# Set-up's segments placed anew, and one sum of the last inner pair rounded by itself, in a two-block transformer kernel

## Chip, cores and metric

One Trainium2 chip; the kernel runs on 1 of its cores. The metric is the device time of one execution in microseconds (us). Each core has TensorE (PE; PEld is its weight load), VectorE (DVE), ScalarE (ACT), GpSimd (POOL) and the DMA queues (SP's above all).

## What is computed

Two model blocks in a row over 512 tokens (plus 16 meta tokens in the first), width 1024. All of it is fp32; the parts that matter here are the square-ReLU MLPs, the gated feed-forward, and the set-up of a state-space filter:

```python
def _sq_relu_mlp(h, w_up, w_down):        # first block, two layers, 4096 inner
    u = jax.nn.relu(h @ w_up)
    return (u * u) @ w_down
# first block: h = h + mixer(rmsnorm(h)); h = h + _sq_relu_mlp(rmsnorm(h), w_up[i], w_down[i])
# second block: attention in three groups, a state-space filter (state 64, 32 groups of 16),
#   a gated feed-forward with 2816 inner, gated embeddings, rmsnorm
```

The state-space filter's tables (powers of a complex decay times B and times C, in chunks of 8 tokens) depend on parameters only. They are computed once, inside the first layer's MLP, where VectorE has room; that is the "set-up".

## The kernel before, in words

**Precision by two halves.** Each fp32 operand is split in a rounded part (`_hi`, fp32r) and the rest (`_lo`); a product is three matmuls, hi by hi, hi by lo, lo by hi (L1303 to L1305). For each unit of weights (128x1024) ACT writes `w_hi` (L2041) and POOL subtracts to get `w_lo` (L1072). For each inner tile of an MLP DVE takes the ReLU out of PSUM (L3670, L3642), ACT squares and rounds it, and DVE subtracts to get the low part (`inner_low`, L3676; `low_inner`).

**The first layer's MLP.** `up00` makes 16 inner tiles (m = 0 to 15), `down00` uses them for 8 output tiles, two units of weights each. PE works tile after tile, with two PSUM banks in turn: tile m + 2 can't start before DVE has taken tile m out of its bank. In `down00`'s first tile PE waits, k by k, for `hidden_lo`, the low part of inner tile k.

**Set-up.** `ssm_setup` (from L3259) is a Python generator of DVE instructions, cut by `yield` into segments. `hidden` (in DVE's `mlp`) emits, for each tile m of `up00`, the ReLU, then one or two segments, then `inner_low`; `plain`, for each tile of `down00`, adds the tile to the residual (L3687) and then emits some segments. DVE carries them out in that written order. Numbered from 0, the segments are: 0 to 10 parameters and angles; 11 to 13 the powers `a_n`; 14 and 15 the table `bb`; 16 to 19 twelve full-width operations (128x1024, three in a segment) that make `pw_re` and `pw_im`, with `ssm_tab` told at the end of 19; 20 the kernel table `kern`; then three with nothing in them (21 to 23); 24 to 35 twelve more full-width operations, one each, that write `pw_re` and `pw_im` again, for C, with `ssm_tab` told after 35; 36 to 38 the powers `a_pow` of the eighth power (small operations). PE waits for segment 19 ahead of `kernel_products`, which it does after `down00`'s tile 1, and DVE in segment 24 waits for PE's transposes of `pw` (`turn_powers`), the last of which follow tile 5. After `down00` comes `first_part`, ten inner tiles whose ReLUs are L3642.

In `up00` tiles 11, 12 and 13 have two segments (11+12, 13+14, 15+16), all other tiles one, so that 17 stands in tile 14 and 18 in tile 15. In `down00`, tiles 0 to 4 have one, tile 5 four (24 to 27), tile 6 five, tile 7 six (33 to 38).

**Down projections by seven products.** Five stretches (parts 0 to 4; the sizes are 10, 12, 12, 10 and 12 inner tiles) do their down projection by a seven-product scheme (Strassen-Winograd) on 2x2 blocks: the inner tiles come in pairs, and a quad is two output tiles, so each part has four quads. The products are called P1, P2, P5, P6, P3, P4, P7, in the order in which PE does them. Inputs on the activation side are seven forms: three are halves of the inner tiles (forms 0 to 2, low parts told by `hidden_lo`), and four are sums s1 to s4 of a pair (forms 3 to 6). DVE makes s1 to s4 (L3564, L3565, L3567, L3568, 128x256 each, or 128x264 in part 0), ACT rounds all four in one instruction (L2434, `sums_high`), and DVE subtracts all four in one (L3556, `sums_low`), which tells `sums_lo`. P5 reads form 3 (s1), P6 reads form 4 (s2), P4 form 2, P7 form 5 and P3 form 6.

In a part's first quad the last pair has only just been made. PE does P1 whole, then P2 and P5 but for the last pair, then P2's last pair, then P5's last pair, then P6 and the others whole. `ready` is the wait for one pair of a product; it is called for P1, P2 and P5 only. DVE's order there is: s1 to s4, the low part of the last inner tile (L3575 or L3579), `keep(P1)` (adds PSUM to the residual, L3550), `sums_low`, `product_low(P6)` (L3531, the low part of the weights of P6), `keep(P2)` and so on. In parts 3 and 4 `product_low(P5)` stands between s4 and the low part. The low weights of P3 and P4 are subtracted on POOL (L1133) after ACT's rounding (L2429).

```python
project(by_name["up00"], hidden)
project(by_name["down00"], plain)
assert not list(setup)
# hidden: for _ in range(2 if m in (11, 12, 13) else 1): next(setup)
# plain:  for _ in range({5: 4, 6: 5, 7: 6}.get(m, 1)): next(setup)
```

Of the kernel before, what the change touches and what calls it, by code (L numbers as in the profile page):

```python
# [48 lines left out]
P1, P2, P5, P6, P3, P4, P7 = range(7)  # L49
# [209 lines left out]
def transposed_blocks_program(nc, a, out):  # L259
# [96 lines left out]
    with ctx:  # L356
# [178 lines left out]
        with ExitStack() as s:  # L535
# [31 lines left out]
            "hidden_full", "hidden_hi", "hidden_lo",  # L567
            "block0", "block1", "block2", "block3", "block4", "block5",
            "weight_sum", "product_hi", "product_lo", "product_lo_pool", "product", "product_kept",
            "pair_sums", "sums_hi", "sums_lo",  # L570
            "gate", "gated", "mixed_hi", "mixed_lo",
            "a_hi", "a_lo", "negmax", "exp", "inverse", "factor", "recip", "last_recip", "eps_rows", "scaled", "probs", "p_full", "p_stored", "metas",
            "dve", "act",
# [49 lines left out]
        def forms_of(part):  # L623
            return (form_hi, form_lo) if part else (first_hi, first_lo)

        def sums_of(part):
            return pair_sums if part else sums_first
# [194 lines left out]
        def bc(t, n):  # L822

            return bass.AP(t.tensor, t.offset, [list(x) for x in t.ap] + [[0, n]])
# [327 lines left out]
        def _(pe):  # L1152
# [500 lines left out]
            def down_by_products(part):  # L1653
# [4 lines left out]

                def ready(i, k):
                    form = PRODUCTS[i][1]  # L1660
                    if form > 2:
                        pe.wait_ge(sems["sums_lo"], FIRST_PAIR[part] + k + 1)
                    else:
                        pe.wait_ge(sems["hidden_lo"], T.at("hidden_lo", 2 * pairs - 1 - 2 * k - (form > 0)))
# [27 lines left out]
                def high(q, i, ks):  # L1692
                    hi, form = weights_of(q, i)[0], PRODUCTS[i][1]
                    opens = i in (P1, P2, P5, P4)
                    for k in ks:
                        if q.first and i in (P1, P2, P5):
                            ready(i, k)
                        mm(region(q, i), hi[:, k, :], forms_hi[:, form, k, :], start=opens and k == 0, stop=False,  # L1698
                           skip_group_check=not opens)
                        mm(region(q, i), hi[:, k, :], forms_lo[:, form, k, :], start=False, stop=False,  # L1700
                           skip_group_check=not opens)
# [323 lines left out]
        def _(act):  # L2025
# [405 lines left out]
            def sums_high(part, j):  # L2431

                act.wait_ge(sems["pair_sums"], FIRST_PAIR[part] + j + 1)
                fn(forms_of(part)[0][:, 3:7, j, :], sums_of(part)[:], ACT.Copy).then_inc(sems["sums_hi"], 1)  # L2434

            def round_inner(part, pair, m):

# [21 lines left out]
            def by_products(part, pj, duty, first=None):  # L2459

                own = [q for q in QUADS if q.part == part]
                instead[BEHIND[part]] = lambda: product_high(own[0], P2)
                project(pj, duty, first=first, carry=True)
                product_high(own[0], P5)
                left_over.pop(0)()
                sums_high(part, PART_SIZES[part] // 2 - 1)
                for q in own:
                    for i in range(7):
                        if not q.first or i > P5:
                            product_high(q, i)  # L2470
                        if part == LAST_PART and i == P5 and not q.first:
                            round_residual(q.before)
                        if q is QUADS[-1] and i == P4:
                            round_p()
                act.wait_ge(sems["product"], own[-1].done(P7) - 2)
                round_unit(BEHIND[part])
                held[BEHIND[part] + 1] = own[-1].done(P7) - 1
                if part == LAST_PART:
                    round_residual(own[-1])
# [406 lines left out]
        def _(dve):  # L2886
# [3 lines left out]
            def step(ins):  # L2890

                ins.then_inc(sems["dve"], T.up("dve"))
                dve.wait_ge(sems["dve"], T.at("dve"))
# [365 lines left out]
            def ssm_setup():  # L3259
# [82 lines left out]
                for part in range(2):  # L3342
# [15 lines left out]
                dve.wait_ge(sems[f"o_full{o}"], T.at(f"o_full{o}"))  # L3358
                v.tensor_tensor(kern[:], ops_[o][:], skip, ALU.add).then_inc(
                    sems[f"o_stored{o}"], T.up(f"o_stored{o}"))  # L3360
                for _ in range(4):
                    yield
                for _ in range(8):
                    others(T, "t_")
# [9 lines left out]
                                yield  # L3374
                v.memset(p(23), 0.0).then_inc(sems["ssm_tab"], T.up("ssm_tab"))
                yield

                pr, pi = a_pow[:, 0], a_pow[:, 1]
                step(v.tensor_copy(pr[:, :, 0:1], re[:, :, 8:9]))
                step(v.tensor_copy(pi[:, :, 0:1], im[:, :, 8:9]))  # L3380
                for n in (1, 2, 4):
                    for _ in product_ops(pr[:, :, n:2 * n], pi[:, :, n:2 * n], pr[:, :, 0:n], pi[:, :, 0:n],
                                         bc(pr[:, :, n - 1], n), bc(pi[:, :, n - 1], n),
                                         *(x[:, :, 0:n] for x in small_t)):
                        pass
                    yield

            setup = ssm_setup()

# [162 lines left out]
            def sums_low(part, j):  # L3552

                dve.wait_ge(sems["sums_hi"], FIRST_PAIR[part] + j + 1)
                hi, lo = forms_of(part)
                v.tensor_tensor(lo[:, 3:7, j, :], sums_of(part)[:], hi[:, 3:7, j, :].bitcast(F32),  # L3556
                                ALU.subtract).then_inc(sems["sums_lo"], 1)

            def sums_of_pair(part, pair):

                t1, t2 = halves_of(part)
                a11, a21, a12, a22 = pair[:, 0, t1], pair[:, 0, t2], pair[:, 1, t1], pair[:, 1, t2]
                s1, s2, s3, s4 = (sums_of(part)[:, n, :] for n in range(4))
                v.tensor_tensor(s1, a21, a22, ALU.add).then_inc(sems["dve"], T.up("dve"))  # L3564
                v.tensor_tensor(s3, a11, a21, ALU.subtract).then_inc(sems["dve"], T.up("dve"))  # L3565
                dve.wait_ge(sems["dve"], T.at("dve", 1))
                step(v.tensor_tensor(s2, s1, a11, ALU.subtract))  # L3567
                v.tensor_tensor(s4, a12, s2, ALU.subtract).then_inc(sems["pair_sums"], 1)  # L3568

# [29 lines left out]
            def by_products(part):  # L3599

                for q in QUADS:
                    if q.part != part:
                        continue
                    if q.first:
                        keep(q, P1)
                        sums_low(part, PART_SIZES[part] // 2 - 1)
                    else:
                        product_low(q, P2)
                        product_low(q, P5)
                        keep(q, P1)  # L3610
                        weight_sum(q, "T4")
                        if part == LAST_PART:
                            low_residual(q.before)
                    product_low(q, P6)
                    keep(q, P2)
                    keep(q, P5)
                    then = None if q.last else QUADS[q.g + 1]
                    keep(q, P6)
                    if then:
                        weight_sum(then, "T3")  # L3620
                    product_low(q, P7)
                    keep(q, P3)
                    if q is QUADS[-1]:
                        low_p()
                    if then:
                        weight_sum(then, "T1")
                        product_low(then, P1)
                    keep(q, P4)
                    if then:
                        weight_sum(then, "T2")  # L3630
                    keep(q, P7)
                    if q is QUADS[-1]:
                        low_residual(q)

            def inner_part(part, pj, pair, banks, factor):
# [3 lines left out]
                def hidden(m, s, t, b):  # L3639
# [6 lines left out]
                    T.saw("hidden_hi")  # L3646
                    if m % 2:
                        dve.wait_ge(sems["hidden_full"], T.at("hidden_full"))
                        sums_of_pair(part, pair)
                    elif m:  # L3650
                        sums_low(part, m // 2 - 1)
                    low_inner(part, pair, m)
# [13 lines left out]
            def mlp():  # L3666
# [11 lines left out]

                def hidden(m, s, t, b):
                    inner(m, s, b)  # L3680
                    for _ in range(2 if m in (11, 12, 13) else 1):
                        next(setup)
                    inner_low(m, s)

                def plain(m, s, t, b):
                    dve.wait_ge(sems[f"full{b}"], T.at(f"full{b}"))
                    store(v.tensor_tensor(h[:, m, :], h[:, m, :], acc1[b], ALU.add), b)  # L3687
                    for _ in range({5: 4, 6: 5, 7: 6}.get(m, 1)):
                        next(setup)

                def hidden_left(m, s, t, b):
# [1 line left out]
                    inner_low(m, s)  # L3693

                project(by_name["up00"], hidden)
                project(by_name["down00"], plain)
                assert not list(setup)
                for name in ("ends_out0", "ends_out1"):
# [457 lines left out]
            for part, pj in ((FFN_PART, ffn_in), (LAST_PART, ffn_rest)):  # L4156
                ahead, tiles = QUADS[part * DT // 2], PART_SIZES[part]

                def ffn(m, s, t, b):
# [10 lines left out]
                        return  # L4170
                    if m % 2:
                        dve.wait_ge(sems["hidden_full"], T.at("hidden_full"))
                        sums_of_pair(part, pair_ffn)
                    if m == tiles - 1:
                        product_low(ahead, P5)
                    low_inner(part, pair_ffn, m)
# [86 lines left out]
```

## Time and profile before

| | |
|---|---|
| median of 3 runs | 2099.0 us (2098.72 to 2099.3) |
| the profiled execution's own time | 2097.7 us |
| its span, first to last instruction | 2095.9 us |
| mean granted TensorE clock | 0.998 |
| PE / PEld / DVE / ACT / POOL busy | 2074.5 / 1819.8 / 1404.1 / 895.7 / 815.2 us |
| HBM traffic over the span | 101 GB/s |

A time in a row is counted from the span's start. A matmul row has its start, its modelled duration, the source line and the operands; matmuls are pipelined, so the distance between two starts, not the duration, says how fast PE issues. A bracket at the end gives the engine's idle time ahead of the instruction and what ended it.

### The profile page before, as it was taken

Reading aid. Unit: us, or ns where it says so; the run is one execution under the profiler, and the core shown is the slowest. Engines: PE = TensorE matmul, PEld = TensorE weight load, DVE = VectorE, ACT = ScalarE, POOL = GpSimd, SP = SyncE. Lnnn points to the kernel's source line nnn. Section 1 sums busy time; section 2 is a strip of 40 time slices with the busy share of each in tenths; the row PEclk is TensorE's granted clock in tenths of the full one; section 3 lists DMA queues with packets and bytes.
Section 4 is the critical chain, followed back from the end, with each engine's and each line's share of the span. In section 5 each row is a group of like instructions: output and inputs, shape, how many; then the busy total and the mean of one; then the engine's idle time right before and its main releaser. Section 6 shows DMA issues by size and latency. Waiting matters only on the chain.

```text
span 2095.9 us, 34962 instructions
## 1 busy us (share of the span) xinstructions
PE 2074.5 (99%) x14218; PEld 1819.8 (87%) x14218; DVE 1404.1 (67%) x2172; ACT 895.7 (43%) x1479; POOL 815.2 (39%) x388
## 2 busy tenths in 40 slices
PE   9999999999999999999999999999999999999998
PEld 9998899999999777798898788888888788988897
DVE  6678766628746395685855769566674577666865
ACT  5368644223435393443434433344433433433344
POOL 3343434344234454423334443333444443344332
PEclk9999999999999999999999999999999999999999
DMA  6620245244233602334343465233333332433341
GB/s 178 169 59 2 57 136 148 84 133 136 73 100 106 188 2 80 102 84 109 81 121 92 131 137 161 67 88 86 91 89 92 91 94 79 120 92 101 89 120 64
DMA packets 375827, 211.23 MB, mean 101 GB/s; under 512 B 27043, under 2 KB 368260, under 8 KB 374776
## 3 DMA queue, kind: packets, MB, share of 16 engines
q1 hardware_dynamic: 365358, 192.62, 32.9%
q10 hardware_dynamic: 10314, 16.41, 2.9%
q8 instruction: 113, 1.85, 0.4%
q14 instruction: 42, 0.34, 0.1%
HBM read 196.97 MB, written 15.40 MB: 101 GB/s over the span
## 4 chain that ended last, share of the span: by engine, by line
PE 62%; issue 22%; POOL 10%; DVE 5%; ACT 1%; DMA 0%; POOLq 0%; SPq 0%; DVEq 0%; ACTq 0%
PE acc L1303 13%; PE acc L1304 13%; PE acc L1305 13%; POOL w_lo L1072 9%; PE acc L1393 2%; PE acc L1708 2%; PE acc L1698 2%; PE acc L1700 2%; PE ops L1462 2%; PE tps L1708 1%; PE tps L1700 1%; PE tps L1698 1%; PE ops L1698 1%; DVE tmp_s L3203 1%; PE ops L1700 1%
## 5 line engine op out<-in xcount | busy, mean ns | idle before, releaser
L1072 POOL TENSOR_TENSOR w_lo<-raw,w_hi 128x1024 fp32r<-128x1024 f32 x270 | 662.0, 2452 | 938.7 <-ACT w_hi L2041 928.2
L2041 ACT ACTIVATE w_hi<-raw 128x1024 fp32r<-128x1024 f32 x269 | 284.8, 1059 | 779.1 <-PE acc L1305 748.5
L1303 PE MATMUL acc<-hr_hi,w_hi 128*128 128x512 f32 x1056 | 421.6, 399 | 0.5 <-DVE qkv L3853 0.3
L1305 PE MATMUL acc<-hr_hi,w_lo 128*128 128x512 f32 x1056 | 417.7, 396 | 0.0
L1304 PE MATMUL acc<-hr_lo,w_hi 128*128 128x512 f32 x1056 | 417.6, 395 | 0.0
L1303 PE MATMUL acc<-hn_hi,w_hi 128*128 128x264 f32 (+1 forms) x840 | 246.8, 294 | 3.3 <-DVE pair_first L3642 2.9
L1305 PE MATMUL acc<-hn_hi,w_lo 128*128 128x264 f32 (+1 forms) x840 | 244.2, 291 | 0.0
L1304 PE MATMUL acc<-hn_lo,w_hi 128*128 128x264 f32 (+1 forms) x840 | 244.2, 291 | 0.0
L1303 PEld LDWEIGHTS acc<-hr_hi,w_hi 128*128 128x128 f32 x1056 | 198.5, 188 | 49.2 <-issue 1.4
L1305 PEld LDWEIGHTS acc<-hr_hi,w_lo 128*128 128x128 f32 x1056 | 198.4, 188 | 47.7
L1304 PEld LDWEIGHTS acc<-hr_lo,w_hi 128*128 128x128 f32 x1056 | 198.5, 188 | 47.3 <-issue 0.7
L1303 PEld LDWEIGHTS acc<-hn_hi,w_hi 128*128 128x128 f32 x840 | 158.2, 188 | 6.6 <-DVE pair_first L3642 3.1
L1304 PEld LDWEIGHTS acc<-hn_lo,w_hi 128*128 128x128 f32 x840 | 158.3, 188 | 2.7
L1305 PEld LDWEIGHTS acc<-hn_hi,w_lo 128*128 128x128 f32 x840 | 157.5, 188 | 2.5
L1303 PE MATMUL acc<-mid_hi,w_hi 128*128 128x264 f32 x352 | 100.6, 286 | 3.9 <-DVE mid_lo L3676 3.2
L1304 PE MATMUL acc<-mid_lo,w_hi 128*128 128x264 f32 x352 | 99.7, 283 | 0.0
L1305 PE MATMUL acc<-mid_hi,w_lo 128*128 128x264 f32 x352 | 99.7, 283 | 0.0
L1133 POOL TENSOR_TENSOR w_lo<-blocks,w_hi 128x768 fp32r<-128x768 f32 (+1 forms) x24 | 44.2, 1848 | 139.0 <-ACT w_hi L2429 139.0
L2429 ACT ACTIVATE w_hi<-blocks 128x768 fp32r<-128x768 f32 (+1 forms) x72 | 58.9, 823 | 86.7 <-PE acc L1708 26.4
L2193 ACT ACTIVATE probs<-probs,stat 128x528 f32<-128x528 f32 (+2 forms) x132 | 85.2, 646 | 13.7 <-DVE stat L3019 13.0
L1095 POOL TENSOR_SCALAR probs<-probs,stat 128x528 f32<-128x528 f32 (+2 forms) x49 | 65.4, 1335 | 61.6 <-DVE stat L3008 61.6
L1303 PEld LDWEIGHTS acc<-mid_hi,w_hi 128*128 128x128 f32 x352 | 66.3, 188 | 4.7 <-DVE mid_lo L3676 3.7
(606 smaller groups left out, 4628.0 us busy)
## 6 DMA issues: line engine op xcount, KB each, us to landing
raw<-in_w_up SPq DMA_DIRECT2D x64, 512.0 KB, 4.9
raw<-in_w_in SPq DMA_DIRECT2D x56, 512.0 KB, 3.8
raw<-in_w_down SPq DMA_DIRECT2D x24, 512.0 KB, 3.7
blocks<-in_w_down SPq DMA_DIRECT2D x32, 384.0 KB, 3.7
raw<-in_w_ffn_gate SPq DMA_DIRECT2D x22, 512.0 KB, 3.8
raw<-in_w_ffn_up SPq DMA_DIRECT2D x22, 512.0 KB, 3.8
raw<-in_w_in_even SPq DMA_DIRECT2D x18, 512.0 KB, 6.9
blocks<-in_w_ffn_down SPq DMA_DIRECT2D x16, 384.0 KB, 3.6
```

What stands on the lines that cost most here:

```text
L1072: nc.gpsimd.tensor_tensor(w_lo[:, part], raw[:, slot], w_hi[:, part].bitcast(F32), ALU.subtract).then_inc(sems["lo"], T.up("lo"))
L1095: nc.gpsimd.tensor_scalar(S, S, st[:, 4:5], None, ALU.mult).then_inc(sems["scaled"], T.up("scaled"))
L1133: nc.gpsimd.tensor_tensor(lo, block_of(q, PRODUCTS[i][0]), hi.bitcast(F32), ALU.subtract).then_inc(sems["product_lo_pool"], 1)
L1303: mm(out, w_hi[:, part, w0 + k, :], xh, start=s0, stop=False)
L1304: mm(out, w_hi[:, part, w0 + k, :], xl, start=False, stop=False)
L1305: ins = mm(out, w_lo[:, part, w0 + k, :], xh, start=False, stop=s1)
L1698: mm(region(q, i), hi[:, k, :], forms_hi[:, form, k, :], start=opens and k == 0, stop=False, skip_group_check=not opens)
L1700: mm(region(q, i), hi[:, k, :], forms_lo[:, form, k, :], start=False, stop=False, skip_group_check=not opens)
L1708: ins = mm(region(q, i), lo[:, k, :], forms_hi[:, form, k, :], start=False, stop=k == pairs - 1, skip_group_check=not opens)
L2041: fn(w_hi[:, n % 2], raw[:, n % 4], ACT.Copy).then_inc(sems["hi"], T.up("hi"))
L2193: fn(S, S, ACT.Exp, bias=st[:, o:o + 1], scale=-1.0, accum_out=p.den(st, o)).then_inc(sems["exp"], T.up("exp"))
L2429: fn(weights_of(q, i)[0], block_of(q, role), ACT.Copy).then_inc(sems["product_hi"], 1)
```

## The change

It has two parts that have nothing to do with each other.

**Set-up.** The segments of `a_pow` (36 to 38) move ahead of the second twelve full-width operations, into the places of segments 21 to 23, which had nothing in them, and the last three places go away. In `up00` tile 13 has one segment instead of two; one segment is emitted between `up00` and `down00`; in `down00` tiles 5, 6 and 7 have 5, 4 and 3 segments. So `up00`'s tile 13 has 15 alone, tile 14 has 16, tile 15 has 17, segment 18 stands after tile 15's `inner_low`, tile 0 has 19 and tile 1 has 20 as before, tiles 2 to 4 have `a_pow`, tiles 5 to 7 the twelve operations, by 5, 4 and 3.

**The last pair's first sum.** For the last pair of each part s1 tells a semaphore of its own (`late_sum`); ACT rounds it by itself (`late_high`) ahead of the other three, and DVE subtracts it by itself (`late_low`), in `by_products` ahead of `keep(P1)`. `sums_high` and `sums_low` of that pair take the other three only. P5's last pair waits for `late_lo`, and P6, in a first quad, now waits pair by pair for `sums_lo`.

```diff
                 def ready(i, k):
                     form = PRODUCTS[i][1]
-                    if form > 2:
+                    if form == 3 and k == pairs - 1:
+                        pe.wait_ge(sems["late_lo"], part + 1)
+                    elif form > 2:
                         pe.wait_ge(sems["sums_lo"], FIRST_PAIR[part] + k + 1)
...
-                        if q.first and i in (P1, P2, P5):
+                        if q.first and i in (P1, P2, P5, P6):
                             ready(i, k)
...
             def sums_high(part, j):
 
                 act.wait_ge(sems["pair_sums"], FIRST_PAIR[part] + j + 1)
-                fn(forms_of(part)[0][:, 3:7, j, :], sums_of(part)[:], ACT.Copy).then_inc(sems["sums_hi"], 1)
+                n = 1 if j == PART_SIZES[part] // 2 - 1 else 0
+                fn(forms_of(part)[0][:, 3 + n:7, j, :], sums_of(part)[:, n:4], ACT.Copy).then_inc(sems["sums_hi"], 1)
+
+            def late_high(part):
+
+                act.wait_ge(sems["late_sum"], part + 1)
+                fn(forms_of(part)[0][:, 3, PART_SIZES[part] // 2 - 1, :], sums_of(part)[:, 0], ACT.Copy).then_inc(
+                    sems["late_hi"], 1)
...
                 left_over.pop(0)()
+                late_high(part)
                 sums_high(part, PART_SIZES[part] // 2 - 1)
...
             def sums_low(part, j):
 
                 dve.wait_ge(sems["sums_hi"], FIRST_PAIR[part] + j + 1)
-                hi, lo = forms_of(part)
-                v.tensor_tensor(lo[:, 3:7, j, :], sums_of(part)[:], hi[:, 3:7, j, :].bitcast(F32),
+                (hi, lo), n = forms_of(part), 1 if j == PART_SIZES[part] // 2 - 1 else 0
+                v.tensor_tensor(lo[:, 3 + n:7, j, :], sums_of(part)[:, n:4], hi[:, 3 + n:7, j, :].bitcast(F32),
                                 ALU.subtract).then_inc(sems["sums_lo"], 1)
 
-            def sums_of_pair(part, pair):
+            def late_low(part):
+
+                (hi, lo), j = forms_of(part), PART_SIZES[part] // 2 - 1
+                dve.wait_ge(sems["late_hi"], part + 1)
+                v.tensor_tensor(lo[:, 3, j, :], sums_of(part)[:, 0], hi[:, 3, j, :].bitcast(F32),
+                                ALU.subtract).then_inc(sems["late_lo"], 1)
+
+            def sums_of_pair(part, pair, late=False):
...
+                if late:
+                    v.tensor_tensor(s1, a21, a22, ALU.add).then_inc(sems["late_sum"], 1)
+                    v.tensor_tensor(s3, a11, a21, ALU.subtract).then_inc(sems["dve"], T.up("dve"))
+                    dve.wait_ge(sems["late_sum"], part + 1)
...
                     if q.first:
+                        late_low(part)
                         keep(q, P1)
                         sums_low(part, PART_SIZES[part] // 2 - 1)
...
-                for _ in range(4):
+                yield
+
+                pr, pi = a_pow[:, 0], a_pow[:, 1]
+                step(v.tensor_copy(pr[:, :, 0:1], re[:, :, 8:9]))
+                step(v.tensor_copy(pi[:, :, 0:1], im[:, :, 8:9]))
+                for n in (1, 2, 4):
...
                     yield
                 for _ in range(8):
                     others(T, "t_")
...
-                    for _ in range(2 if m in (11, 12, 13) else 1):
+                    for _ in range(2 if m in (11, 12) else 1):
                         next(setup)
...
-                    for _ in range({5: 4, 6: 5, 7: 6}.get(m, 1)):
+                    for _ in range({5: 5, 6: 4, 7: 3}.get(m, 1)):
                         next(setup)
...
                 project(by_name["up00"], hidden)
+                next(setup)
                 project(by_name["down00"], plain)
```

The old `a_pow` code at the generator's end is taken out, and the two callers of `sums_of_pair` pass `m == tiles - 1` as `late`.

## Rows read from the trace of the kernel before

**Rows 1.** The page, part 1: busy time, share of the span, instructions

```profile
PE 2074.5 (99%) x14218; PEld 1819.8 (87%) x14218; DVE 1404.1 (67%) x2172; ACT 895.7 (43%) x1479; POOL 815.2 (39%) x388
```

**Rows 2.** Waits of PE over the span: total us, times, longest us

```profile
PE acc L1303 <- DVE mid_lo L3676: 3.2, 2, 2.7
PE acc L1303 <- DVE pair_first L3642: 2.9, 1, 2.9
...
PE acc L1303 <- DVE hid L3670: 0.6, 1, 0.6
```

**Rows 3.** Timeline of PE from up00's end to first_part: start us, duration us

```profile
377.61 0.28 PE L1305 MATMUL acc<-hn_hi,w_lo 128*128 128x264 f32 x1
378.51 0.39 PE L1303 MATMUL acc<-mid_hi,w_hi 128*128 128x264 f32 x1 [0.63 <-DVE hid L3670]
...
389.36 0.28 PE L1305 MATMUL acc<-mid_hi,w_lo 128*128 128x264 f32 x1
392.32 0.39 PE L1303 MATMUL acc<-mid_hi,w_hi 128*128 128x264 f32 x1 [2.68 <-DVE mid_lo L3676]
...
404.85 0.43 PE L1582 MATMUL ops<-pw_re,ct_re 128*32 128x128 f32 x8
...
495.02 0.39 PE L1303 MATMUL acc<-hn_hi,w_hi 128*128 128x264 f32 x1 [2.89 <-DVE pair_first L3642]
```

**Rows 4.** Timeline of DVE, 371 to 400 us: set-up's full-width operations

```profile
371.28 2.48 DVE L3203 TENSOR_TENSOR tmp_s<-bb,a_n 128x1024 f32<-128x1024 f32 x2
373.80 3.30 DVE L3203 TENSOR_TENSOR pw_re<-tmp_s 128x1024 f32<-128x1024 f32 x1
...
391.56 0.71 DVE L3676 TENSOR_TENSOR mid_lo<-hid,mid_hi 128x528 fp32r<-128x528 f32 x1
...
398.56 1.22 DVE L3203 TENSOR_TENSOR pw_im<-tmp_s 128x1024 f32<-128x1024 f32 x1
```

**Rows 5.** Timeline of POOL, at the second of those rows

```profile
373.27 2.75 POOL L1072 TENSOR_TENSOR w_lo<-raw,w_hi 128x1024 fp32r<-128x1024 f32 x1 [3.22 <-ACT w_hi L2041]
```

**Rows 6.** Timeline of DVE at down00's end and first_part's start

```profile
487.14 0.16 DVE L3379 COPY a_pow<-a_n 128x16 f32<-128x16 f32 x1
...
494.26 0.71 DVE L3642 SCALAR_TENSOR_TENSOR pair_first<-acc,rstd 128x528 f32<-128x528 f32 x1 [0.23 <-DVE a_pow L3203]
```

**Rows 7.** Timeline of PE in the first quads of parts 0, 3 and 4

```profile
546.53 0.29 PE L1708 MATMUL tps<-first_hi,w_lo 128*128 128x264 f32 x1
547.36 0.39 PE L1698 MATMUL ops<-first_hi,w_hi 128*128 128x264 f32 x1 [0.54 <-DVE first_lo L3556]
...
1784.29 0.28 PE L1708 MATMUL tps<-form_hi,w_lo 128*128 128x256 f32 x1
1785.41 0.39 PE L1698 MATMUL ops<-form_hi,w_hi 128*128 128x256 f32 x1 [0.85 <-DVE form_lo L3556]
...
1970.92 0.28 PE L1708 MATMUL tps<-form_hi,w_lo 128*128 128x256 f32 x1
1971.21 0.39 PE L1698 MATMUL ops<-form_hi,w_hi 128*128 128x256 f32 x1
```

**Rows 8.** Timeline of DVE in the first quad of part 3

```profile
1783.21 0.69 DVE L3575 TENSOR_TENSOR form_lo<-hid,form_hi 128x512 fp32r<-128x512 f32 x1
1783.81 0.41 DVE L3550 TENSOR_TENSOR h<-h,acc 128x256 f32<-128x256 f32 x1
1784.14 1.22 DVE L3556 TENSOR_TENSOR form_lo<-pair_sums,form_hi 128x1024 fp32r<-128x1024 f32 x1
1785.28 0.82 DVE L3531 TENSOR_TENSOR third_lo<-blocks,third_hi 128x640 fp32r<-128x640 f32 x1
```

**Rows 9.** Timelines of ACT and POOL in the same quad

```profile
1782.59 1.06 ACT L2434 ACTIVATE form_hi<-pair_sums 128x1024 fp32r<-128x1024 f32 x1 [0.96 <-DVE pair_sums L3568]
...
1785.48 3.58 POOL L1133 TENSOR_TENSOR w_lo<-blocks,w_hi 128x640 fp32r<-128x640 f32 x2 [13.59 <-ACT w_hi L2429]
```

**Rows 10.** Waits of all engines: ACT on a DMA of raw weights

```profile
ACT w_hi L2041 <- DMA raw<-in_w_up: 9.4, 3, 4.1
```

More of the change, by code:

```diff
@@ L569, in transposed_blocks_program @@
             "weight_sum", "product_hi", "product_lo", "product_lo_pool", "product", "product_kept",
-            "pair_sums", "sums_hi", "sums_lo",
+            "pair_sums", "sums_hi", "sums_lo", "late_sum", "late_hi", "late_lo",
             "gate", "gated", "mixed_hi", "mixed_lo",
@@ L3360, in ssm_setup @@
                     sems[f"o_stored{o}"], T.up(f"o_stored{o}"))
-                for _ in range(4):
+                yield
[3 more added lines that the diff above has]
+                for n in (1, 2, 4):
+                    for _ in product_ops(pr[:, :, n:2 * n], pi[:, :, n:2 * n], pr[:, :, 0:n], pi[:, :, 0:n],
+                                         bc(pr[:, :, n - 1], n), bc(pi[:, :, n - 1], n),
+                                         *(x[:, :, 0:n] for x in small_t)):
+                        pass
                     yield
@@ L3376, in ssm_setup @@
                 yield
[L3378 to L3386, printed above, removed]
             setup = ssm_setup()
@@ L3563, in sums_of_pair @@
                 s1, s2, s3, s4 = (sums_of(part)[:, n, :] for n in range(4))
-                v.tensor_tensor(s1, a21, a22, ALU.add).then_inc(sems["dve"], T.up("dve"))
-                v.tensor_tensor(s3, a11, a21, ALU.subtract).then_inc(sems["dve"], T.up("dve"))
-                dve.wait_ge(sems["dve"], T.at("dve", 1))
+                if late:
+                    v.tensor_tensor(s1, a21, a22, ALU.add).then_inc(sems["late_sum"], 1)
+                    v.tensor_tensor(s3, a11, a21, ALU.subtract).then_inc(sems["dve"], T.up("dve"))
+                    dve.wait_ge(sems["late_sum"], part + 1)
+                else:
+                    v.tensor_tensor(s1, a21, a22, ALU.add).then_inc(sems["dve"], T.up("dve"))
+                    v.tensor_tensor(s3, a11, a21, ALU.subtract).then_inc(sems["dve"], T.up("dve"))
+                    dve.wait_ge(sems["dve"], T.at("dve", 1))
                 step(v.tensor_tensor(s2, s1, a11, ALU.subtract))
@@ L3648, in hidden @@
                         dve.wait_ge(sems["hidden_full"], T.at("hidden_full"))
-                        sums_of_pair(part, pair)
+                        sums_of_pair(part, pair, m == tiles - 1)
                     elif m:
@@ L4172, in ffn @@
                         dve.wait_ge(sems["hidden_full"], T.at("hidden_full"))
-                        sums_of_pair(part, pair_ffn)
+                        sums_of_pair(part, pair_ffn, m == tiles - 1)
                     if m == tiles - 1:
```

## The prediction

> **What bounds the kernel now.** The page's busy times come first: PE is busy for 2074.5 of 2095.9 us [rows 1], everything else far less. So a change pays only where it takes away a wait of PE, and the next view is the list of PE's waits. Three of its entries belong to set-up: PE waited for `mid_lo` (2.7 us of the 3.2 in one wait), for `pair_first` (2.9) and for `hid` (0.6) [rows 2]. Each is DVE being late, and the timeline shows where [rows 3]. At 378.51 us `down00`'s first matmul waits for the ReLU of `up00`'s tile 14 to leave its bank. At 392.32 the low part of inner tile 15, the last, is awaited. At 495.02 `first_part`'s third tile waits for the ReLU of its first. The true cost of a wait is the distance between starts less the usual one of 0.12 us: 378.51 - 377.61 - 0.12 = 0.78; 392.32 - 389.36 - 0.12 = 2.84; for the third I take the bracket, 2.89, plus the 0.16 by which the other two exceed theirs, 3.05. Together 6.67 us.
>
> The timeline of the first quads gives the other part [rows 7]: P5's last pair starts 0.71 us late in part 0 (547.36 - 546.53 - 0.12), 1.00 in part 3, 0.17 in part 4. In parts 1 and 2 I found no such gap. Together 1.88 us, so 8.55 us of PE's waiting are in reach.
>
> **Why DVE is late in set-up.** From 371 us on, DVE has no idle time. A full-width operation takes 1.22 to 1.24 us alone (2.48 for two; 1.22), but 3.30 when it meets POOL [rows 4]: it began at 373.80 inside POOL's subtraction of 373.27 and ended at 377.10, 1.08 after POOL had ended at 376.02 [rows 5]. So a segment of three costs 3.70 us, and 2.1 more for each meeting. There is one POOL subtraction per unit of weights, every 5.8 us or so while PE isn't held up. The Trainium skill ("SBUF — State Buffer", section on the two separate sides) says that the pair of ports shared by the two engines is held for a whole instruction by whichever began first, and the other fully blocks; by that rule the operation would end at 376.02 + 1.22 = 377.24, and the trace agrees within 0.14 us.
>
> **The queue after the change, step by step.** Tile 14 of `up00` is full at about 371.95 (tile 15 ends at 377.61 + 0.12, less a tile of 5.8). DVE by then has only done segment 15. From 371.95 its order is ReLU 14, segment 16, low 14, ReLU 15, segment 17, low 15, segment 18, addition of tile 0, segment 19. A ReLU, a low part or an addition takes 0.65 to 0.71 [rows 4, 6]; I count 0.65, since instructions overlap a little.
> - ReLU 15: 371.95 + 0.65 + 3.70 + 2.1 + 0.65 + 0.65 = 379.7. The ReLU of tile 14, for which `down00` waited, is done at 372.6: 0.78 us are gone. `down00`'s first tile starts at 377.73.
> - Low 15: 379.7 + 3.70 + 0.65 and two meetings (POOL's subtractions near 379 and 385) = 388.2. PE wants it at 392.32 - 2.84 - 0.78 = 388.7. It comes 0.5 us early, so the 2.84 are gone, narrowly.
> - Segments 18 and 19: 388.2 + 7.40 + 0.65 and two meetings = 400.5. `kernel_products` started at 404.85 [rows 3] and would now want `ssm_tab` at 404.85 - 3.62 = 401.2. It fits by 0.7 us.
>
> That last margin is a wait that the change moves: segment 19 stays in tile 0, but 18 is now queued ahead of it there. Behind both, DVE's additions of tiles 1 and 2 have a whole tile of some 12 us each.
>
> **The tail of set-up.** DVE now ends the last tile's segments with the `a_pow` ones, from 487.14 to the ReLU at 494.26 [rows 6]: 7.1 us, which go to tiles 2 to 4, where segments had nothing in them and DVE does only a 0.7 us addition per tile. Tiles 5, 6, 7 hold the same twelve operations, one more in tile 5, one fewer in 6 and the same three in 7. The ReLU comes at about 487.3 (less all shifts), and PE, which would reach that tile at 495.02 - 3.05 = 492.0, needs its bank 4 us after the ReLU is done. The 3.05 us are gone in full. What is late next: nothing by these rows; ACT squares this tile right behind.
>
> The extra instructions of the placement are none: it only moves them. Set-up's sum: -6.67.
>
> **The first sum by itself.** Added per part are one ACT instruction, one DVE instruction, their waits, and PE's waits ahead of P6's pairs. ACT sat idle for 0.96 us ahead of the rounding of the four sums [rows 9]. A rounding a quarter as wide as its 1.06 us fits there, so I cost it at nothing. If that cover went, it would cost at most 1.06. On DVE a 256-wide operation advances the queue by 0.33 (1783.81 to 1784.14), a 1024-wide one by 1.14 (1784.14 to 1785.28) [rows 8]; each further 256 of width by (1.14 - 0.33) / 3 = 0.27, so three quarters of the width by 0.33 + 2 x 0.27 = 0.87. In part 3:
> - `late_low` 1783.81 to 1784.22; P5's last pair is wanted at 1784.29 + 0.12 = 1784.41. The 1.00 is gone.
> - `keep(P1)` 1784.14 to 1784.56, wanted by P6's opening at 1784.76 + 0.12 = 1784.88.
> - `sums_low` of three 1784.47 to about 1785.4; P6 wants its last pair at 1784.88 + 8 x 0.12 = 1785.8.
> - `product_low(P6)` from 1785.34, ending 0.82 later at 1786.16. P6's low weights are now wanted at 1784.88 + 10 x 0.12 = 1786.1: a new wait of some 0.1 us, and what was 1.00 yields 0.9.
>
> In parts 0 and 4 the same steps leave 0.4 us or more at each place (there PE was late by less), so 0.71 and 0.17. In parts 1 and 2 I count nothing. PE's new waits for pairs made long ago: P5 has them already and issues at 0.12 all the same, so nothing. Sum: -1.78.
>
> **Forecast.** -6.67 - 1.78 = -8.45 against the profiled execution's 2097.7, that is 2089.3. The median shown is 1.3 above that execution, so 2099.0 - 8.4 = **2090.6 us**. A measurement of this kernel can tell about 0.2% (4.2 us) from no change.
>
> **Rivals.**
> 1. *DVE's queue takes one meeting more.* The margins of 0.5 and 0.7 us are smaller than one meeting, 2.1. Then `mid_lo` is awaited for 1.6 us, or `kernel_products` for 1.4, or both in part: 2092.2. For it: DVE had no idle time there. Against: meetings are bound to POOL's subtractions, one each 5.8 us, and I counted five of them. Chance 0.13.
> 2. *The first sum gives nothing*, since the wait moves from P5 to P6's opening, or `late_high` isn't ahead of the rest on ACT after all: 2099.0 - 6.7 = 2092.3. Against it: the steps above. Chance 0.07.
> 3. *The time comes back later*, at something not paced by PE. ACT waited 9.4 us in three waits for a DMA of raw weights [rows 10]; if arrivals in a later stage were set by the memory and not by freed buffers, PE would run into them 8 us earlier. With 5 to 8 us given back: 2095.6 to 2099. Against it: the DMAs move 101 GB/s over the span and are issued as buffers come free. Chance 0.07.
> 4. *The port goes to POOL first, and the kernel is slower.* In part 3 DVE began `product_low(P6)` at 1785.28 and POOL its subtractions at 1785.48 [rows 8, 9]. By my steps DVE now begins at 1785.34. The point that decides is a further 0.14 us: if POOL begins first, DVE ends 0.82 after POOL's 1.8 (one subtraction) or 3.58 (both), so PE waits 2.0 or 3.8 us. In part 3 alone that gives 2090.6 + 2 to 4 = 2092.6 to 2094.5. In all five parts with both subtractions it gives 5 x 3.8 = 19 against the 6.7 of set-up: 2111, slower. Chance 0.06 for one part, 0.02 for enough of them to be slower than before. The same section of the skill makes this rival possible: by its rule whoever begins first decides, and the sum above is the case in which DVE does.
>
> **How the numbers follow.** The forecast has what is left, 0.65, with its own range of 2089.6 to 2092.0 (all waits gone with nothing new: 2099.0 - 8.55 = 2090.4, and 0.8 below that for wake-ups after a wait that I left out and for the spread of runs; upwards the two narrow margins). Rivals 1 and 2 and the one-part case of 4 lie up to 2094.5, so the range 2089.6 to 2094.6 holds all but rival 3 and the slower case. Faster by over 0.2% means below 2094.8: 0.65 + 0.13 + 0.07 + 0.06 = 0.91. Within 0.2%: 0.07. Slower: 0.02.
>
> **What would show it.** In the changed kernel's list of PE's waits `hid`, `mid_lo` (but for the 0.5 us of the second wait) and `pair_first` should be gone, and those for `form_lo` and `first_lo` too. `kernel_products` should start at about 401.2 and `down00`'s first matmul at 377.7. The small `a_pow` operations should lie in `down00`'s tiles 2 to 4. In part 3 PE should show a gap of at most 0.2 us ahead of P6's low products, with DVE's subtraction begun before POOL's. I am wrong if PE's wait for `ssm_tab` or for the low weights of P6 exceeds 1 us, or if a wait that isn't in the list of before takes more than 1 us anywhere.

## The result and the profile after

The changed kernel takes 2087.6 us (median of 5; 2086.9 to 2087.8), the one before 2099.0 (2098.7 to 2099.3): 11.4 us or 0.54% less between the medians; the ratio over all runs is 0.9944 with a 95% interval of 0.9931 to 0.9958, which doesn't take in 1. The forecast was 2090.6 with a range of 2089.6 to 2094.6: the sign was right, the time lies 2 us below the range. The profiled execution took 2087.2, its span is 2085.4.

The changed kernel's list of PE's waits, whole (total us, times, longest us), against [rows 2]:

```profile
PE ops L1990 <- DVE sq L4247: 1.9, 1, 1.9
PE acc L1491 <- DVE sq_tok L3113: 1.1, 1, 1.1
PE acc L1393 <- issue: 0.9, 1, 0.9
PE acc L1303 <- DVE mid_lo L3698: 0.6, 1, 0.6
PE ops L1434 <- DVE mix_e_lo L3071: 0.5, 2, 0.3
PE tps L1402 <- ACT probsT L2208: 0.5, 1, 0.5
PE acc L1303 <- POOL w_lo L1072: 0.5, 2, 0.3
PE acc L1235 <- DVE hn_lo L3130: 0.3, 1, 0.3
PE tps L1402 <- issue: 0.2, 1, 0.2
```

`pair_first`, `hid` and the long `mid_lo` are gone, and so are `form_lo` and `first_lo`. PE at the places of [rows 3]: `down00`'s first matmul, its last k, that is the product with inner tile 15 (389.36 and 392.32 before), and `kernel_products`.

```profile
376.84 0.29 PE L1303 MATMUL acc<-mid_hi,w_hi 128*128 128x264 f32 x1
...
387.59 0.28 PE L1305 MATMUL acc<-mid_hi,w_lo 128*128 128x264 f32 x1
387.71 0.28 PE L1303 MATMUL acc<-mid_hi,w_hi 128*128 128x264 f32 x1
...
400.13 0.43 PE L1582 MATMUL ops<-pw_re,ct_re 128*32 128x128 f32 x8
```

PE now passes the last k at its usual 0.12 us. `down00` starts 0.89 us ahead of the 377.73 that the forecast had, and `kernel_products` 1.1 ahead of its 401.2; 0.9 of it was gained before `down00` begins, at two places that no change touched (below). DVE in the same stretch, against [rows 4] (start us, duration us):

```profile
371.86 4.56 DVE L3213 TENSOR_TENSOR tmp_s<-bb,a_n 128x1024 f32<-128x1024 f32 x2
376.46 1.22 DVE L3213 TENSOR_TENSOR pw_re<-tmp_s 128x1024 f32<-128x1024 f32 x1
...
378.96 4.06 DVE L3213 TENSOR_TENSOR tmp_s<-bb,a_n 128x1024 f32<-128x1024 f32 x2
...
384.32 2.79 DVE L3698 TENSOR_TENSOR mid_lo<-hid,mid_hi 128x528 fp32r<-128x528 f32 x1
387.03 2.47 DVE L3213 TENSOR_TENSOR tmp_s<-bb,a_n 128x1024 f32<-128x1024 f32 x2
...
391.42 3.94 DVE L3213 TENSOR_TENSOR tmp_s<-bb,a_n 128x1024 f32<-128x1024 f32 x2
395.40 1.23 DVE L3213 TENSOR_TENSOR pw_im<-tmp_s 128x1024 f32<-128x1024 f32 x1
396.70 0.07 DVE L3359 MEMSET par<- 128x16 f32 x1
```

The low part of tile 15 is done at 387.11 and wanted at 387.71: 0.6 us to spare, where the forecast had 0.5. Segment 19 ends at 396.77 and is wanted at 400.13: 3.4 to spare instead of 0.7. Most of the difference is in the meetings with POOL, which cost 2.1, 1.6, 2.1, 0 and 1.5 us (4.56 - 2.48, 4.06 - 2.48, 2.79 - 0.71, 0, 3.94 - 2.48) and not five times 2.1. The 0 is POOL's subtraction of 389.78, which began inside a DVE operation: there POOL waited, taking 3.25 us instead of about 2.4.

The first quad of part 3, against [rows 7, 8, 9]: DVE, POOL and PE.

```profile
1774.39 0.42 DVE L3572 TENSOR_TENSOR form_lo<-pair_sums,form_hi 128x256 fp32r<-128x256 f32 x1
1774.73 0.41 DVE L3559 TENSOR_TENSOR h<-h,acc 128x256 f32<-128x256 f32 x1
1775.06 0.95 DVE L3565 TENSOR_TENSOR form_lo<-pair_sums,form_hi 128x768 fp32r<-128x768 f32 x1
1775.92 0.82 DVE L3540 TENSOR_TENSOR third_lo<-blocks,third_hi 128x640 fp32r<-128x640 f32 x1
...
1776.07 3.63 POOL L1133 TENSOR_TENSOR w_lo<-blocks,w_hi 128x640 fp32r<-128x640 f32 x2 [13.62 <-ACT w_hi L2431]
...
1774.87 0.28 PE L1710 MATMUL tps<-form_hi,w_lo 128*128 128x256 f32 x1
1774.98 0.28 PE L1700 MATMUL ops<-form_hi,w_hi 128*128 128x256 f32 x1
...
1776.40 0.28 PE L1702 MATMUL acc<-form_lo,third_hi 128*128 128x256 f32 x1
1776.80 0.85 PE L1710 MATMUL acc<-form_hi,third_lo 128*128 128x256 f32 x5
```

P5's last pair follows at 0.11 us where it was 1.00 late. DVE began P6's low weights 0.15 us ahead of POOL. They ended at 1776.74, so PE started on them 0.28 us late (1776.80 - 1776.40 - 0.12), and lost 0.24 more in the matmuls behind.

**Where the traces differ.** I paired every matmul of the one trace with the same matmul of the other and read the difference of their starts. It grows by 0.88 at `down00`'s start, 2.95 at its last k, 3.15 in `first_part` (7.0 for set-up); by 0.8 in part 0, 0.1 in parts 1 and 2, 0.6 net in part 3 (1.12 less 0.52), 0.3 in part 4 (1.8 for the sums). That is 8.8 us at the forecast's places, for 8.45 forecast. Another 1.7 lies where no instruction was changed or moved: 0.4 in the first 13 us, 0.5 at 343 us (a wait for POOL), 0.6 at 1282 us, 0.2 between 1800 and 1831 us (there in the trace of the placement alone too, in which the sums are as before). Together that is the 10.5 us between the two spans. So of the medians' 11.4 us, the trace of before gives the change 8.8, and 2.6 are open.

### The profile page after: what moved, and what is told of

It is laid out like the page before. It is cut to its first block, busy times and chain, and to the rows that moved or that the text cites. A ratio compares the mean times of both kernels' runs of the same rounds, so it can differ in the third digit from the quotient of the medians.

```text
span 2085.4 us, 34976 instructions
## 1 busy us (share of the span) xinstructions
PE 2072.4 (99%) x14218; PEld 1819.1 (87%) x14218; DVE 1404.8 (67%) x2177; ACT 898.2 (43%) x1484; POOL 820.0 (39%) x388
## 4 chain that ended last, share of the span: by engine, by line
PE 70%; issue 18%; POOL 8%; DVE 2%; ACT 1%; DMA 0%; SPq 0%; POOLq 0%; DVEq 0%; ACTq 0%
PE acc L1303 15%; PE acc L1304 15%; PE acc L1305 15%; POOL w_lo L1072 8%; PE acc L1393 2%; PE ops L1462 2%; PE acc L1710 2%; PE acc L1702 2%; PE acc L1700 2%; PE tps L1710 1%; PE tps L1700 1%; PE tps L1702 1%; PE tps L1402 1%; PE acc L1176 1%; PE ops L1700 1%
## 5 line engine op out<-in xcount | busy, mean ns | idle before, releaser
L3533 DVE TENSOR_TENSOR blocks<-blocks 128x768 f32<-128x768 f32 (+1 forms) x64 | 63.0, 989 | 12.2 <-POOL w_lo L1133 9.4
```

The source lines that it names most:

```text
L3533: v.tensor_tensor(block_of(q, role), block_of(q, x), block_of(q, y), ALU.subtract).then_inc(sems["weight_sum"], 1)
```

## The experiments

The theory at this point (A) is that the listed waits are the whole effect and the two parts add. The first four runs take the change apart.

**Set-up's placement alone.** The generator and its counts as changed; the sums as before:

```diff
-                    for _ in range(2 if m in (11, 12, 13) else 1):
+                    for _ in range(2 if m in (11, 12) else 1):
...
+                next(setup)
...
-                    for _ in range({5: 4, 6: 5, 7: 6}.get(m, 1)):
+                    for _ in range({5: 5, 6: 4, 7: 3}.get(m, 1)):
```

> Set-up's placement alone, the sums as before. Theory A (the three waits in set-up and their wake-ups are the whole effect of this part, and the two parts of the change add): 6.9 us faster than before by the trace (0.87 to 0.9 at the start of down00, 2.95 at its last k, 3.1 to 3.2 in first_part), waits of about 0.71, 1.0 and 0.17 us for the last sums still there. Theory B (PE's earlier arrival also removes waits further on, as the 0.3 us one for qkv at 1282 us): 0.6 more, and that wait gone in this run's trace. Theory C (the timed executions of the kernel before hold waits that its one profiled execution doesn't): the difference of medians exceeds that of the traces by about 0.9 us here, and not in the run of the sums alone.

Measured: 2088.8 us (2088.7 to 2089.6), the kernel before 2098.3 beside it (27 runs, 2095.8 to 2101.1), so -9.5; ratio 0.9958 (0.9945 to 0.9972). In the trace the three places give 0.88, 2.95 and 3.15, as in the whole change. The wait at 1282 us is gone here, which speaks for B, but it is gone in the next three traces as well, also where only the sums were changed. Theory C's sign is there: the medians differ by 9.5 us and the spans of the two traces by 8.6 (2095.9 and 2087.3), 0.9 more. So the timed executions of before hold something that its one trace doesn't; that it is a wait, as C says, no trace shows.

**The first sum alone.** The edits of `ready`, `sums_high`, `late_high`, `late_low`, `sums_low` and `sums_of_pair` of the change, with set-up as before.

> The first sum by itself, alone. Theory A: 2.0 us faster (0.8 in part 0, 0.05 in parts 1 and 2 each, 1.1 less a new wait of 0.2 to 0.45 in part 3, 0.3 in part 4), and with the placement alone it adds up to the whole change within 0.5 us. Theory B or C: the whole change is faster than the two single parts together by 1 us or more.

Measured: 2097.3 (11 runs, 2094.6 to 2099.0), -1.0 where A had -2.0; ratio 0.9997 (0.9988 to 1.0006), which can't be told from no change. With the placement alone it adds up to 10.5, 0.9 short of the whole change's 11.4, between A's 0.5 and the 1 of B and C, so this run decides between none of them. In its trace the last sums' waits are gone as expected, and the new wait of 0.28 in part 3 is there.

**The tail of set-up alone.**

```diff
-                    for _ in range({5: 4, 6: 5, 7: 6}.get(m, 1)):
+                    for _ in range({5: 5, 6: 4, 7: 3}.get(m, 1)):
```

with `a_pow`'s segments ahead of the twelve operations.

> Only the a_pow segments moved ahead of the second twelve operations, with 5, 4 and 3 segments in down00's tiles 5 to 7; up00 as before. Theory A: 3.1 us faster, the wait of 2.9 for pair_first gone, those for hid (0.6) and mid_lo (2.7) unchanged. Rival: the wait for pair_first only shrinks, since DVE meets POOL once more in tile 7: 1 us faster or less.

Measured: 2093.9 (2092.7 to 2097.6), -4.4; ratio 0.9983 (0.9974 to 0.9992). The wait for `pair_first` is gone, the other two stand, and the rival (1 us or less) fell.

**The head alone.**

```diff
-                    for _ in range(2 if m in (11, 12, 13) else 1):
+                    for _ in range(2 if m in (11, 12) else 1):
...
                 project(by_name["up00"], hidden)
+                next(setup)
```

> Only one segment of up00's tile 13 taken behind tile 15, down00 with 4, 5 and 6 segments and a_pow last, as before. Theory A: 3.8 us faster, the waits for hid and mid_lo gone, that for pair_first (2.9) unchanged. Rival (down00's queue hands it on): kernel_products waits for ssm_tab by 1 us or more and the gain is under 3 us.

Measured: 2093.8 (2091.8 to 2094.6), -4.5; ratio 0.9979 (0.9970 to 0.9988). `hid` and the long `mid_lo` are gone, `pair_first` stands. The rival fell: `kernel_products` waits for nothing.

Two things stood out. Tail and head gain 4.4 and 4.5 where the waits taken away were 3.15 and 3.8, and set-up as a whole 9.5 for 7.0. And every kernel so far that keeps a wait of 2.8 us or more (by the starts) has times spread over 3 to 5 us, those without one over 1 us. Behind such waits, the traces of these runs have a stretch that the first trace of before has not: PE issues a matmul every 0.22 us or so instead of 0.12, at a granted clock of 0.50. The run of the tail alone shows it in two windows of 1 us, behind the wait for `mid_lo` that ends at 391.62 (columns as in the windows further down):

```profile
392.00:393.00 1.00, 1.00 (x11) 1.00 (x10) 0.35 (x1) 0.35 (x1) 0.00 (x0) 1.00 0.72 215
393.00:394.00 1.00, 1.00 (x7) 1.00 (x7) 1.00 (x2) 0.71 (x1) 0.21 (x1) 0.51 0.00 0
```

That such a fall of the clock is part of the price of a wait is theory D. Rival E is that a wait costs its length alone. Four runs test it, two of them the kernel before itself.

**A short wait of chosen length**, in the changed kernel:

```diff
                 project(by_name["down00"], plain)
                 assert not list(setup)
+                for _ in range(3):
+                    tt(tmp_s[:, 0], tmp_s[:, 0], tmp_s[:, 1], ALU.subtract)
```

> The changed kernel with three more full-width operations (128x1024) on DVE between down00 and first_part's first ReLU, whose results nobody reads: a wait of PE of a chosen length at the place where the kernel before waits for pair_first. Theory D (a wait of about 3 us costs its length, and in some executions 1.4 to 1.6 us more, because TensorE's granted clock falls from 1.00 to 0.50 for a stretch behind it): here PE waits about 1.9 us, no stretch at 0.50, and the time is 1.5 to 2.5 us over the changed kernel's with as little spread (about 1 us). Rival E (a wait costs its length alone, and the 3 us by which the change gained more than forecast come from the start of the executions): the same here.

Measured: 2089.9 (5 runs, 2089.4 to 2091.1), 2.3 over the changed kernel. PE's wait was 1.8 us by the list, 1.95 by the starts, and the granted clock behind it 1.00 in the profiled execution, the fastest of the five:

```profile
489.30:491.30 2.00, 2.00 (x16) 2.00 (x17) 0.90 (x2) 1.97 (x3) 0.00 (x0) 1.00 0.04 11
```

The spread is 1.7 us and not about 1: two of the five took 2091.0 and 2091.1, which one fall would give. So that a wait of this length never has a fall is not shown. The changed kernel was not taken again beside this and the later runs; "over the changed kernel" is over its 2087.6.

**A long wait**: the same with `range(6)`.

> The same with six more operations: PE waits about 8 us there. Theory D: always a stretch at 0.50 behind the wait, so 9 to 10.5 us over the changed kernel. Rival E: 7.5 to 8.5 us over it, no stretch.

Measured: 2095.4 (10 runs, 2095.05 to 2096.2), 7.8 over the changed kernel. As written, that lies in E's range. But the wait was 5.95 us by the list, 6.1 by the starts, and not 8, so neither sum holds as written. With the true length rival E gives 6.1, theory D 7.5 to 7.7, and a stretch at 0.50 is there, 9 matmuls in the first 2 us:

```profile
493.30:495.30 2.00, 2.00 (x9) 2.00 (x10) 0.90 (x2) 1.97 (x3) 0.00 (x0) 0.50 0.00 0
```

The ten times lie within 1.2 us, as they would if every execution had its fall.

**The kernel before, profiled again, twice** (no edit).

> The kernel before, another profiled execution. Theory D: the waits of 2.7 and 2.9 us stand as in the first profile, and behind one or both of them, in some executions, the granted clock is 0.50 for a stretch, worth 1.4 to 1.6 us each. Further: the short waits at 343 us (0.4, for POOL) and 1282 us (0.5, for DVE) that only the first profile of the kernel before had are not here, 0.9 us less. Rival E: clock 1.00 behind both, and the span is within 1 us of the first profile's, up or down by what the first 20 us take.

> The kernel before once more, the same expectations as for the first look: of the two looks theory D wants at least one stretch at 0.50 behind one of the waits (each of the three single-part runs that kept such waits had one behind 3 of 4 of them); rival E wants none.

Measured: 2100.2 (span 2098.4) and 2098.6 (span 2096.8), against 2097.7 (2095.9) in the first profile. In what follows these are the second and the third profile. The two stretches behind the waits for `mid_lo` and `pair_first` by windows (us; busy us and count of PE, PEld, DVE, ACT, POOL; granted clock; DMA share, GB/s), of the kernel before in its first profile, then in the third:

```profile
392.40:394.40 2.00, 2.00 (x17) 2.00 (x18) 1.04 (x2) 1.04 (x1) 0.00 (x0) 1.00 0.57 171
495.10:497.10 2.00, 2.00 (x17) 2.00 (x18) 0.97 (x2) 1.92 (x3) 0.00 (x0) 1.00 0.02 4
```

```profile
392.40:394.40 2.00, 2.00 (x11) 2.00 (x11) 1.09 (x2) 1.06 (x1) 0.00 (x0) 0.50 0.23 68
498.00:500.00 2.00, 2.00 (x11) 2.00 (x11) 1.47 (x1) 1.15 (x2) 2.00 (x1) 0.50 0.33 135
```

PE is busy throughout in all four and does 17 matmuls at 1.00 (2.4 GHz) and 11 at 0.50 (1.2 GHz). What a fall costs is read from the first matmul behind the wait to `kernel_products`. In the first profile that was 404.85 - 392.32 = 12.53 us [rows 3]. The second and the third profile have:

```profile
391.26 0.59 PE L1303 MATMUL acc<-mid_hi,w_hi 128*128 128x264 f32 x1 [2.64 <-DVE mid_lo L3676]
...
406.60 0.43 PE L1582 MATMUL ops<-pw_re,ct_re 128*32 128x128 f32 x8
```

```profile
391.59 0.59 PE L1303 MATMUL acc<-mid_hi,w_hi 128*128 128x264 f32 x1 [2.66 <-DVE mid_lo L3676]
...
405.48 0.43 PE L1582 MATMUL ops<-pw_re,ct_re 128*32 128x128 f32 x8
```

that is 15.34 and 13.89, 2.8 and 1.4 us more for the same work. The short waits at 343 and 1282 us are in neither, as expected: they were chance in the first profile. Theory D holds and E falls. In all thirteen traces the granted clock is at 0.50 nowhere else between 20 us and the last 10 us of the span. In the three single-part runs that kept such waits, all four waits had a fall behind them.

The timed executions of the kernel before say the same. Beside the runs it was timed 57 times: 11 executions with a mean granted clock of 0.996 took 2099.5 to 2101.1 us, 27 with 0.997 took 2097.1 to 2099.8, and 19 with 0.998 took 2095.3 to 2098.0. (The mean also takes in the last 5 to 8 us, which are at 0.50 in every trace; it sorts the executions, it doesn't count their falls.)

The Trainium skill ("TensorE: Matmul & The Clock Gate", Part 1) says that idling sends TensorE back from its upper clock level to the lower; by that rule each long wait can have such a price behind it, and these traces agree that it is behind waits that the clock falls. Which length is enough is read from the rows of this case alone.

**A wait in between**: three operations and one of half the width.

```diff
+                tt(tmp_s[:, 0, 0:4], tmp_s[:, 0, 0:4], tmp_s[:, 1, 0:4], ALU.subtract)
```

> As e5_wait_short with one more operation of half the width: PE waits about 2.5 us for pair_first. It narrows down which waits let the clock fall: at 1.95 us it did not, at 2.8 to 3.05 us it did in 8 of 10. Theory D: 2.5 us over the changed kernel without a fall, or 4 with one; runs that have it and runs that haven't lie 1.5 us apart, so the spread is wider than the 1 us of the changed kernel. Rival E: 2.5 us over it and as narrow.

Measured: 2091.2 (6 runs, 2090.0 to 2091.9), 3.6 over the changed kernel. The profiled execution is the fastest of them (2090.0), has the wait (2.52 us) and no fall. The others being up to 1.9 us slower is what falls would give, and the mean granted clock points the same way (0.999 in the two fastest, 0.998 or 0.997 in the four others), but no trace shows one, so it stays open for this length.

**The margin of tile 15's low part**: one segment more ahead of it.

```diff
-                    for _ in range(2 if m in (11, 12) else 1):
+                    for _ in range(2 if m in (11, 12, 15) else 1):
...
-                next(setup)
                 project(by_name["down00"], plain)
```

> The changed kernel with segment 18 ahead of the low part of up00's last tile instead of behind it. It measures the margin that the forecast put at 0.5 us: the low part comes three full-width operations later (3.7 us, and 0 to 2.1 for meeting POOL), so PE waits 3.1 to 5.2 us for mid_lo in down00's first tile. Theory D adds a stretch at 0.50 behind it, 1.4 to 1.6 us: 4.5 to 6.8 us over the changed kernel, and segment 19 still in time for kernel_products. Rival E: 3.1 to 5.2 us over it.

Measured: 2092.5 (9 runs, 2091.6 to 2093.2), 4.9 over the changed kernel. The wait, and the stretch behind it, in this kernel's timeline and windows:

```profile
391.73 0.39 PE L1303 MATMUL acc<-mid_hi,w_hi 128*128 128x264 f32 x1 [3.06 <-DVE mid_lo L3698]
```

```profile
393.00:395.00 2.00, 2.00 (x11) 2.00 (x11) 1.97 (x3) 0.84 (x1) 1.09 (x1) 0.50 0.00 0
```

By the starts the wait is 3.2 us, and the 60 matmuls behind it take 8.91 us where 7.37 is usual: 3.2 + 1.5 = 4.7. The 4.9 lies in the ranges of both theories; what speaks for D is the stretch. So one segment in the wrong place costs 4.9 us, a third of it behind the wait.

**The new wait of part 3.** P6 in two halves, its low weights ahead of the sums:

```diff
+                    if q.first:
+                        open_product(q, P6)
+                        for ks in (most, rest):
+                            high(q, P6, ks)
+                            low(q, P6, ks)
...
                         keep(q, P1)
+                        product_low(q, P6)
                         sums_low(part, PART_SIZES[part] // 2 - 1)
```

> The changed kernel, and in each first quad P6 is done as P2 and P5 are: all pairs but the last with high and low weights, then the last; DVE subtracts P6's low weights ahead of the three sums instead of behind them. By the steps of the trace of the changed kernel (part 3: the subtraction would end about 1775.9 us, wanted 1776.4; the sums 1776.8, wanted 1776.9) the wait of 0.28 us for those weights and the 0.25 us behind it go: 0.5 us faster in the trace, nothing that the times can tell. Rival: the three sums are then late for the last pair, and the wait only changes its name, 0 us or slower by up to 0.3.

Measured: 2087.5 (2087.4 to 2087.8), the changed kernel's time. In part 3 the wait for the low weights is gone, and P3 now opens 0.29 us late behind a `keep` on DVE that the same queue has pushed back:

```profile
1777.77 0.28 PE L1710 MATMUL acc<-form_hi,third_lo 128*128 128x256 f32 x1
1778.18 0.36 PE L1700 MATMUL ops<-form_hi,w_hi 128*128 128x256 f32 x1
```

The span is 2085.6 us for 2085.4. The wait changed its name, though not the name that the rival gave it: the three sums were in time. This is no version that beats the changed kernel, and none of the runs is.

## Why the prediction was wrong

**What bounds the kernel, and the waits.** Right. All five listed waits went, at their places. For set-up 6.67 was forecast and the trace has 7.0; the 0.3 more is the 0.1 that PE loses behind each wait, which the forecast had left out. For the sums 1.78 was forecast and the trace has 1.8, by luck: 0.8, 0.1, 0.6 and 0.3 us in parts 0, 1 and 2, 3 and 4 stand against 0.71, 0, 0.90 and 0.17. The two parts act apart from each other: the placement alone has the same three steps as the whole change.

**The step that failed** is "the true cost of a wait is the distance between starts less the usual one of 0.12 us". For the waits of 2.8 to 3.05 us it is not. Behind such a wait the granted clock falls to 0.50 for a stretch in most executions. Six profiled executions kept one or two of these waits, ten in all (two in each of the three of before and in the run of the first sum alone, one each in tail and head). Eight of the ten had a fall, and the two without one are both in the first profile of before. Behind each fall 60 matmuls took 8.7 to 8.9 us instead of 7.4, once 10.2. The mean over the ten is 1.3 us, so 2.6 for the two waits of before. 8.8 + 2.6 = 11.4 us, what the medians show. That it comes out to the tenth is luck: beside the later runs the kernel before took 2098.3, 2098.5 and 2097.8, which is 10.2 to 10.9 over the changed kernel's 2087.6, so the sum is good to about 1 us. The same sum fits the parts: tail 3.15 + 1.3 = 4.45 (measured 4.4), set-up 7.0 + 2.6 = 9.6 (9.5), head 3.8 + 1.3 = 5.1 (4.5).

The execution profiled before had no fall at all, and every term was read from it; how many of the timed ones are such isn't known. The forecast saw that the median was 1.3 us above it and carried that over as a constant, though it was part of what the change would take away. By the traces those 1.3 us are about 2.6 of falls that this execution lacked, less about 1.6 us that it had by chance at its start, at 343 and at 1282 us and that the second and third profile have not.

**The queue.** The margin of 0.5 us for the low part of tile 15 was 0.6. Segment 19's was 3.4 and not 0.7, since a meeting with POOL costs what is left of POOL's instruction, and not always 2.1 us. Rival 1 did not come: no further meeting. With margins of 0.5 and 0.7 us against a meeting of 2.1 it could have, and what a late low part costs is the 4.9 us of the run above.

**The tail.** Right: DVE was done with `pair_first`'s first ReLU about 4 us before PE needed the bank. The small operations lie in tiles 2 to 4 and cost nothing.

**The first sum.** Right in place; the new wait ahead of P6's low weights cost 0.52 us and not 0.1. The forecast counted one distance of 0.12 too many ahead of P6: three matmuls of P5's last pair after 1784.41 make 1784.76 and not 1784.88, so the weights were wanted that much earlier. PE started 0.28 late, and the matmuls after a wait come at larger distances for a while (0.23 us for the first instead of 0.12). Rival 2 fell.

**The port.** DVE did begin ahead of POOL in part 3, by 0.15 us where the forecast had 0.14. It wasn't luck of one execution: in the five other traces with this order of instructions (the first sum alone, the three runs with added waits, tile 15's low part) it is 0.14 as well. Rival 4's point of decision was met on the side that I had taken; what the other side costs wasn't tried. Rival 3 fell: no new wait of more than 1 us appeared anywhere.

## What to carry to other kernels

A wait of TensorE near 3 us is worth more than its length: here 1.3 us more on average. Where only some executions pay it, the times spread over 3 to 5 us; behind the longer waits of 3.2 and 6.1 us they spread over 1.6 and 1.2. Before pricing a wait from one trace, look at the granted clock behind it in two or three executions, and take a median above the profiled time, or a wide spread, as a sign that the trace may lack what most executions have. When an in-order queue feeds two consumers, ask for each instruction who needs it and by when: one segment moved behind one low part was worth 4.9 us here, though the queue's work stayed the same.

## What the runs showed of the hardware

- After a wait of 1.8 or 2.5 us (by the list) the granted clock stayed at 1.00 in the one profile of each, and the spread of the timed runs (1.7 and 1.9 us) leaves open whether it always does; after ten of 2.6 to 2.9 it fell to 0.50 in eight, after 3.06 and 5.95 in the one profile of each.
- A fall cost 1.4 to 1.6 us; once, in the second profile of before, it lasted about twice as long and cost 2.8. The one of the 6.1 us wait lasted as long, but began in the wait, and cost 1.3 behind it.
- The fall need not come at the wait: in five of the ten falls PE had already worked 0.8 to 1.5 us at 1.00 again before the clock fell (1.4 in the run of the tail alone), in the other five the clock was at 0.50 when PE resumed.
- The first matmul after a wait is followed by the next at 0.23 us instead of 0.12, so even a wait without a fall costs 0.1 us over its length.
- A full-width DVE operation or a low part that begins while POOL subtracts loses from 1.5 to 2.2 us (2.2 at 388.11 us in the trace of before, 3.42 instead of 1.22), according to how much of POOL's instruction is left. The ReLU at 378.35 and the addition at 390.80 in the trace of the changed kernel, which read PSUM, took their usual 0.70 us inside POOL's subtractions.
